# Token halves at four norms, context first at a fifth, shorter GpSimd sums behind two blocks

## The chip, the cores and the metric

The kernel runs on one core of one Trainium2 chip. The metric is the device time of one execution in microseconds (us), the median of three runs. The engines are named as in the profile: PE (TensorE), DVE (VectorE), ACT (ScalarE), POOL (GpSimd), SP (the queue that issues most transfers).

## What is computed

Two network blocks on 256 latent tokens of width 1024; the second also carries 256 context tokens. Cut to what matters here:

```python
h = rms_norm(x, norm_g) * (1 + scale) + shift      # before every projection
x = x + gate * y                                   # after every mixer: the residual
lat = lat + 0.5 * mod[:, 0, 2] * _swiglu(_modulate(lat, ...), w13, w2)   # FFN of 2816 hidden
cx  = cx  + 0.5 * modc[0, 2]   * _swiglu(_modulate(cx,  ...), w13, w2)   # the same weights
```

All of it is float32. `scale`, `shift` and `gate` of each layer come from matrix-vector products of the condition vector with `ada_w` and `mod_w`. The norm's mean runs over the 1024 features of one token, so a norm can't start until every feature of that token has its residual, and tokens do not depend on each other there.

## The kernel before

**Layout.** Activations are held transposed: XT has 8 chunks of 128 features (k = 0 to 7) by 512 tokens, the latent tokens in columns 0 to 255, the context tokens in 256 to 511. Each float32 product is made of three matmuls on rounded halves: weights split into Wh and Wl, activations into Hh and Hl (`three`, L1320: Wh·Hh, Wh·Hl, Wl·Hh).

**Stages.** 17 linear stages run one after the other: even_in, even_out, odd_in, odd_out, ffn0_up, ffn0_down, conv_in, conv_out, ffn1_up, ffn1_down, ffn2_up, ffn2_down, gqa_kv, gqa_q, gqa_out, ffn3_up, ffn3_down (table STAGES, L44). The stages from ffn0_up to gqa_kv work on 512 tokens, the others on 256. A stage is a row of weight tiles. A tile of 2048 columns holds two output blocks by 8 input chunks: 48 matmuls. A tile of an FFN down stage holds half of the hidden chunks of one output block: 33 matmuls, and two tiles make one output chunk. One number per stage in the table, `gemv`, says how many rows of the modulation products DVE takes beside each tile (`modulation_of`, L870): each is two dot products of 1024 elements (`dot`, L855, lines L864 and L867, or one at L861 for the first block).

**The path of a tile.** SP loads it into raw (two slots), ACT copies it, rounded, into Wh (`split`, L527), DVE subtracts to get Wl (L832), PE multiplies. There are two Wh/Wl slots; the next tile is split while PE works on this one, and ACT's split of tile n waits until PE is through with tile n-2.

**A norm.** `splits` (ACT, L561) squares each chunk of XT once its residual is written; POOL adds the squares of the first chunks into tmp[2] (L460, count in SUMMED, L257); PE multiplies that sum and the squares of the remaining chunks with a column of ones into psN (`sum_of`, L1378); DVE makes the means (L897), POOL takes them to the power -1/2 (L452), PE spreads the result over 128 rows (`spread`, L1376), then for each chunk DVE scales (`scaled`, L903), ACT adds the shift and rounds (L586), DVE makes the low part (L919), all helpers' DVE operations under L819. PE's first tile of the next stage takes chunk by chunk. The norm ffn0_up also folds the first block's final norm in (L890 to L894, L467, and at the end 8 rescalings of XT, L921). The residuals are made on DVE in `residual` (L925) and `ffn_down` (L960).

**Order.** Each engine runs one hand-written list, at the end of its block; semaphores connect them. On DVE, the step of a tile is: split of the next tile, modulation products, residual of this tile.

## Time and profile before

| | |
|---|---|
| median of 3 runs | 2079.53 us (2076.51 to 2079.58) |
| the profiled execution, its own time | 2075.76 us |
| its span | 2073.9 us |
| PE busy | 1906.5 us, 92% |
| DVE busy | 1397.0 us, 67% |
| ACT busy | 689.9 us, 33% |
| POOL busy | 128.0 us, 6% |
| granted TensorE clock, mean | 0.965 |
| bytes moved | 315.79 MB, mean 152 GB/s |

Busy shares are means over stages with different limits. A matmul's duration in the trace overlaps with the next one's, so the time per matmul is read from start to start, or as a piece of the chain divided by its instructions.

### The profile page before, as it was taken

To read this page: it belongs to the slowest core of one execution; us is meant where nothing else is said; L and a number is where in the kernel's file an instruction comes from. 1 tells how busy PE (TensorE), PEld (TensorE's weight loads), DVE (VectorE), ACT (ScalarE), POOL (GpSimd) and SP (SyncE) were. 2 spreads that over 40 slices of the span, in tenths; PEclk is the share of its full clock that TensorE was granted. 3 is DMA by queue.
4 is the path that set the end of the run, shared out by engine and by line. 5 is a ranking of instruction groups with operands and counts; after the bars stand their busy time and mean duration, and the time that the engine had idled before them with its cause. 6 is when DMAs were issued, how large, how long until landed. Compare 5 with 4: busy or idle time off the path is not lost.

```text
span 2073.9 us, 26722 instructions
## 1 busy us (share of the span) xinstructions
PE 1906.5 (92%) x10092; PEld 1621.9 (78%) x10092; DVE 1397.0 (67%) x2081; ACT 689.9 (33%) x926; POOL 128.0 (6%) x78
## 2 busy tenths in 40 slices
PE   2986799799999998998999999999999998879998
PEld 2955788688888877876888888778888887669998
DVE  7878899876666666668666666676665226755554
ACT  2454355422222223332222222232222213444432
POOL 2001200200000110003000001100000010010000
PEclk9987899799999999998999999999999999999999
DMA  9843854423443452334333444433343233223444
GB/s 378 319 169 78 227 199 176 174 105 138 152 152 133 157 187 112 136 138 171 118 131 146 152 144 155 178 114 132 148 152 108 96 110 113 83 82 142 168 160 158
DMA packets 75738, 315.79 MB, mean 152 GB/s; under 512 B 19060, under 2 KB 22904, under 8 KB 56344
## 3 DMA queue, kind: packets, MB, share of 16 engines
q1 hardware_dynamic: 75136, 314.15, 42.7%
q8 instruction: 37, 0.61, 0.1%
q10 hardware_dynamic: 536, 0.79, 0.1%
q14 instruction: 29, 0.24, 0.0%
HBM read 313.86 MB, written 1.06 MB: 152 GB/s over the span
## 4 chain that ended last, share of the span: by engine, by line
PE 74%; DVE 18%; ACT 3%; issue 2%; DMA 1%; POOL 1%; SPq 0%; DVEq 0%; ACTq 0%
PE acc L1318 72%; DVE Wl L832 4%; ACT Wh L527 2%; DVE tmp L819 2%; PE psN L1318 1%; DVE psGT L861 1%; DVE psGT L867 1%; DVE psGT L864 1%; DVE najunk L867 1%; DVE najunk L864 1%; DVE small L989 1%; DVE XT L819 1%; DMA afirst<-in_ada_w 1%; PE psN L1380 1%; DVE tmp L1007 1%
## 5 line engine op out<-in xcount | busy, mean ns | idle before, releaser
L1318 PE MATMUL acc<-Hh,Wh 128*128 128x512 f32 (+1 forms) x2320 | 808.4, 348 | 48.7 <-DVE Hl L819 23.3
L1318 PE MATMUL acc<-Hl,Wh 128*128 128x512 f32 (+1 forms) x2320 | 799.5, 345 | 0.0
L1318 PE MATMUL acc<-Hh,Wl 128*128 128x512 f32 (+1 forms) x2320 | 798.9, 344 | 0.0
L832 DVE TENSOR_TENSOR Wl<-raw,Wh 128x2048 fp32r<-128x2048 f32 (+1 forms) x214 | 449.6, 2101 | 270.3 <-ACT Wh L527 270.2
L1318 PEld LDWEIGHTS acc<-Hh,Wh 128*128 128x128 f32 x2320 | 447.9, 193 | 112.9 <-issue 46.7
L527 ACT ACTIVATE Wh<-raw 128x2048 fp32r<-128x2048 f32 (+1 forms) x214 | 374.3, 1749 | 343.0 <-PE acc L1318 329.6
L1318 PEld LDWEIGHTS acc<-Hl,Wh 128*128 128x128 f32 x2320 | 448.5, 193 | 50.4 <-issue 0.7
L1318 PEld LDWEIGHTS acc<-Hh,Wl 128*128 128x128 f32 x2320 | 447.4, 193 | 50.5
L1318 PE MATMUL acc<-hidh,Wh 128*128 128x512 f32 (+1 forms) x704 | 258.6, 367 | 0.9 <-DVE Wl L832 0.9
L1318 PE MATMUL acc<-hidl,Wh 128*128 128x512 f32 (+1 forms) x704 | 258.3, 367 | 0.0
L1318 PE MATMUL acc<-hidh,Wl 128*128 128x512 f32 (+1 forms) x704 | 258.2, 367 | 0.0
L594 ACT ACTIVATE tmp<-acc 128x512 f32<-128x512 f32 (+1 forms) x88 | 47.9, 544 | 454.6 <-PE acc L1318 454.6
L819 DVE SCALAR_TENSOR_TENSOR tmp<-tmp,acc 128x512 f32<-128x512 f32 (+1 forms) x176 | 109.3, 621 | 131.1 <-ACT tmp L594 120.9
L460 POOL TENSOR_TENSOR tmp<-tmp 128x512 f32<-128x512 f32 (+1 forms) x44 | 93.2, 2118 | 1308.4 <-ACT tmp L558 1151.5
L864 DVE SCALAR_TENSOR_TENSOR psGT<-graw,cb 128x1024 f32<-128x1024 f32 x122 | 167.7, 1375 | 0.4
L867 DVE SCALAR_TENSOR_TENSOR psGT<-graw,cb 128x1024 f32<-128x1024 f32 x122 | 154.9, 1270 | 4.2
L1318 PEld LDWEIGHTS acc<-hidh,Wh 128*128 128x128 f32 x704 | 132.4, 188 | 24.8 <-DVE Wl L832 1.1
L1318 PEld LDWEIGHTS acc<-hidh,Wl 128*128 128x128 f32 x704 | 132.4, 188 | 24.0
L1318 PEld LDWEIGHTS acc<-hidl,Wh 128*128 128x128 f32 x704 | 132.4, 188 | 23.9
L956 DVE TENSOR_TENSOR hidl<-tmp,hidh 128x512 f32 (+3 forms) x88 | 55.1, 626 | 71.4 <-ACT hidh L597 71.4
L819 DVE SCALAR_TENSOR_TENSOR XT<-acc,mod,XT 128x256 f32 (+3 forms) x88 | 36.0, 455 | 88.5 <-PE acc L1318 88.5
L597 ACT ACTIVATE hidh<-tmp 128x512 f32 (+3 forms) x88 | 50.9, 578 | 133.5 <-DVE tmp L819 133.5
(222 smaller groups left out, 1187.7 us busy)
## 6 DMA issues: line engine op xcount, KB each, us to landing
raw<-in_ffn_up SPq DMA_DIRECT2D x88, 1024.0 KB, 4.8
graw<-in_mod_w SPq DMA_DIRECT2D x144, 512.0 KB, 5.5
raw<-in_ffn_down SPq DMA_DIRECT2D x64, 704.0 KB, 4.1
graw<-in_ada_w SPq DMA_DIRECT2D x32, 512.0 KB, 5.7
raw<-in_odd_in SPq DMA_DIRECT2D x16, 1024.0 KB, 4.9
raw<-in_even_in SPq DMA_DIRECT2D x12, 1024.0 KB, 7.0
raw<-in_conv_in SPq DMA_DIRECT2D x12, 1024.0 KB, 4.8
afirst<-in_ada_w SPq DMA_DIRECT2D x8, 1024.0 KB, 13.0
```

The lines of the kernel that those rows point to most:

```text
L460: nc.gpsimd.tensor_tensor(tmp[:, 2, 0:n], tmp[:, 0 if k == 1 else 2, 0:n], tmp[:, k % 2, 0:n], ALU.add).then_inc(n_sum, 1)
L527: nc.scalar.activation(Wh[:, half, 0:f], raw[:, slot, 0:f], ACT.Copy).then_inc(hi_ready, 1)
L594: nc.scalar.activation(tmp[:, b, 0:s.tokens], acc[b][0][:, 0:s.tokens], ACT.Tanh, scale=0.5)\
L597: nc.scalar.activation(at3(hidh, t, s.tokens), tmp[:, 3, 0:s.tokens], ACT.Copy).then_inc(ffn_hi, 1)
L819: return nc.vector.scalar_tensor_tensor(out=out, in0=a, scalar=s, in1=b, op0=op0, op1=op1)
L832: nc.vector.tensor_tensor(Wl[:, half, 0:f], raw[:, slot, 0:f], Wh[:, half, 0:f].bitcast(f32), ALU.subtract)\
L861: nc.vector.scalar_tensor_tensor(out=psGT[:, :], in0=graw[:, slot, :], scalar=0.5, in1=cfirst[:, :], op0=ALU.mult, op1=ALU.mult, accum_out ...
L864: nc.vector.scalar_tensor_tensor(out=junk[:, :], in0=graw[:, slot, :], scalar=0.5, in1=cb[:, 0, :], op0=ALU.mult, op1=ALU.mult, accum_out= ...
L867: nc.vector.scalar_tensor_tensor(out=junk[:, :], in0=graw[:, slot, :], scalar=0.5, in1=cb[:, 1, :], op0=ALU.mult, op1=ALU.mult, accum_out= ...
L956: nc.vector.tensor_tensor(at3(hidl, t, c), tmp[:, 3, c], at3(hidh, t, c).bitcast(f32), ALU.subtract)\
L989: link(nc.vector.tensor_reduce(out=out, in_=L[:, u % 2, :, :], op=ALU.max, axis=AX.X))
L1318: return nc.tensor.matmul(out, lhsT, rhs, start=start, stop=stop)
```

## The change

It has five parts.

1. **Halved tokens** at the norms conv_in, ffn1_up, ffn2_up and gqa_kv (`HALVED`). The last output tile of the stage before is computed for the latent tokens first (semaphore lat_done), then for the context tokens. The latent half's residual, last squares, sums, power and spread run while PE is in the context half. The next stage's first two tiles are then taken as: latent tokens of tile 0, of tile 1, context tokens of tile 0, of tile 1, and DVE and ACT do the latent chunks first, then the context chunks. The matmuls concerned have 256 columns in place of 512. The splits of the next stage's first tiles are cut into halves of 1024 columns and put between the chunks.
2. **Context first** at the norm ffn0_up. The context rows' norm is known since the norm odd_in, so the context halves of the first two tiles are normed and multiplied first, and the sums and power of the latent tokens run beside. The 8 rescalings of XT stand after the stage ffn0_up.
3. **Sums** behind even_out and odd_out (`MID`): POOL adds four chunks' squares (3 additions for 5), and PE takes chunks 4 and 5 itself, inside the last tile, after its sixth input chunk.
4. **Products**: conv_out takes 1 modulation row per tile for 2, gqa_out 1 for 0.
5. **Splits** of tile 2 of ffn0_up, ffn1_up and ffn2_up are put behind the tanh of tile 0 on ACT, and before the low part of tile 0 on DVE.

```diff
-    ("conv_out", 4, 16, 0, TOK, 2, "dve"),
+    ("conv_out", 4, 16, 0, TOK, 1, "dve"),
...
-    ("gqa_out", 4, 16, 0, LAT, 0, "dve"),
+    ("gqa_out", 4, 16, 0, LAT, 1, "dve"),
...
-        SUMMED = {"even_in": 6, "odd_in": 5, "ffn0_up": 5, "conv_in": 6, "ffn1_up": 5, "ffn2_up": 6, "gqa_kv": 6, "ffn3_up": 5}
+        SUMMED = {"even_in": 6, "odd_in": 3, "ffn0_up": 3, "conv_in": 6, "ffn1_up": 5, "ffn2_up": 6, "gqa_kv": 6, "ffn3_up": 5}
...
+        HALVED = {n: i for i, n in enumerate(["conv_in", "ffn1_up", "ffn2_up", "gqa_kv"])}
+        LAST = {n: (KC - 2, KC - 1) if n == "ffn1_up" else (KC - 1,) for n in HALVED}
+        CL, CC = slice(0, LAT), slice(LAT, TOK)
```

DVE at a halved norm:

```diff
+                dve.wait_ge(lat_done, l + 1)
+                residual_half(0, CL).then_inc(lat_res, 1)
+                meanwhile()
+                mean(0, psN, lat_ss, l + 1).then_inc(lat_mean, 1)
+                if not ffn:
+                    split(S[name].n0)
+                dve.wait_ge(lat_spread, l + 1)
+                scaled(0, 0, CL, psN).then_inc(lat_t, 1)
+                for k in range(KC):
+                    if k + 1 < KC:
+                        if k > 0:
+                            dve.wait_ge(lat_ready, KC * l + k)
+                        scaled(k + 1, 0, CL, psN).then_inc(lat_t, 1)
+                    if ffn and k < 2:
+                        split_half(S[name].n0, k)
+                    dve.wait_ge(lat_hi, KC * l + k + 1)
+                    low(k, 0, CL).then_inc(lat_ready, 1)
+                    if k in (5, 7):
+                        split_half(S[name].n0 + 1, k // 2 - 2)
+                    if k == 2:
+                        dve.wait_ge(tile_done, s.n0 + s.tiles)
+                        residual_half(1, CC).then_inc(drained["dve"], 1)
+                    if k == 5:
+                        mean(1, psT[1], n_ss, i + 1).then_inc(n_mean, 1)
```

PE at a halved norm, the last tiles of an FFN down stage and the first two of the next stage:

```diff
+                    part(0, 0, CL)
+                    sum_of_sums(name)
+                    part(0, 1, CL).then_inc(lat_done, 1)
+                    part(1, 0, CC, lat_sums).then_inc(tile_done, 1)
+                    lat_spreads(name)
+                    part(1, 1, CC).then_inc(tile_done, 1)
...
+                pe.wait_ge(lo_ready, s.n0 + 1)
+                part(0, CL, lat_ready, KC * l, {3: ctx_sums, 7: ctx_spread})
+                pe.wait_ge(lo_ready, s.n0 + 2)
+                pe.wait_ge(drained["dve"], prev.drained1)
+                part(1, CL, lat_ready, KC * l, {})
+                part(0, CC, h_ready, H0[name], {}).then_inc(tile_done, 1)
+                part(1, CC, h_ready, H0[name], {}).then_inc(tile_done, 1)
```

PE behind even_out and odd_out, and at the norm ffn0_up:

```diff
+                        if k == 5 and X_TO.get(s.name) in MID and t == s.tiles - 1:
+                            sums_between(X_TO[s.name])
...
+            part(0, CC, ctx_ready, 0, range(4))
+            for k in range(KC - 2, KC):
+                pe.wait_ge(n_sq, KC * i + k + 1)
+                ins = sum_of("ffn0_up", tmp[:, k % 2, :], False, k == KC - 1)
+            ins.then_inc(n_ss, 1)
+            part(0, CC, ctx_ready, 0, range(4, KC))
+            pe.wait_ge(lo_ready, s.n0 + 2)
+            pe.wait_ge(drained["dve"], S["odd_out"].drained1)
+            part(1, CC, ctx_ready, 0, range(4))
+            pe.wait_ge(n_rstd, i + 1)
...
+            part(1, CC, ctx_ready, 0, range(4, KC))
+            part(0, CL, h_ready, H0["ffn0_up"], range(KC)).then_inc(tile_done, 1)
+            part(1, CL, h_ready, H0["ffn0_up"], range(KC)).then_inc(tile_done, 1)
```

**The order of the work, place 1: PE between ffn0_down and conv_in.** Before, the last tile runs to its end, then come the squares' sums, the spread, and the first matmul of conv_in:

```order
L1318 MATMUL acc<-hidh,Wl 128x512
L1380 MATMUL psN<-ones,tmp 128x1 [waits n_sq]
L1380 MATMUL psN<-ones,tmp 128x1 x3
L1376 MATMUL psN<-ident,rstd 128x128 [waits n_rstd]
L1376 MATMUL psN<-ident,rstd 128x128 x3
```

Now sums and spread of the latent tokens (psN) stand inside the context half of the last output chunk (hidh, hidl are the FFN's hidden values):

```order
L1523 MATMUL acc<-hidh,Wl 128x256
L1559 MATMUL psN<-ones,tmp 128x1 [waits lat_sq]
L1559 MATMUL psN<-ones,tmp 128x1
L1523 MATMUL acc<-hidh,Wh 128x256
```

```order
L1523 MATMUL acc<-hidh,Wl 128x256
L1675 MATMUL psN<-ident,rstd 128x128 [waits lat_rstd]
L1675 MATMUL psN<-ident,rstd 128x128
L1523 MATMUL acc<-hidh,Wh 128x256 [waits lo_ready]
```

15 matmuls stand between lat_done and the sums, 18 more between the sums and the spread, 33 behind the spread.

**Place 2: DVE at the conv_in norm.** Before, the whole split of tile 1 (2048 columns) stands ahead of the first scaled chunk, and both halves of a chunk follow each other:

```order
L819 SCALAR_TENSOR_TENSOR XT<-acc,mod,XT 128x256 [waits tile_done]
L819 SCALAR_TENSOR_TENSOR XT<-acc,mod,XT 128x256
L897 TENSOR_SCALAR means<-psN 128x4 [waits n_ss]
L819 SCALAR_TENSOR_TENSOR mod<-mod,vec 128x16 [waits g_taken]
L832 TENSOR_TENSOR Wl<-raw,Wh 128x2048 [waits hi_ready,dve_chain]
L819 SCALAR_TENSOR_TENSOR tmp<-XT,mod,psN 128x256 [waits n_spread]
L819 SCALAR_TENSOR_TENSOR tmp<-XT,mod,psN 128x256 x3
L819 SCALAR_TENSOR_TENSOR Hl<-tmp,mod,Hh 128x256 [waits n_hi]
```

Now the latent chunks are alone, with the half splits (128x1024) of tiles 0 and 1 and the context residual between them:

```order
L909 SCALAR_TENSOR_TENSOR XT<-acc,mod,XT 128x256 [waits lat_done]
L909 SCALAR_TENSOR_TENSOR mod<-mod,vec 128x16 [waits g_taken]
L998 TENSOR_SCALAR means<-psN 128x2 [waits lat_ss,dve_chain]
L909 SCALAR_TENSOR_TENSOR tmp<-XT,mod,psN 128x256 [waits lat_spread]
L909 SCALAR_TENSOR_TENSOR tmp<-XT,mod,psN 128x256
L982 TENSOR_TENSOR Wl<-raw,Wh 128x1024 [waits hi_half]
L909 SCALAR_TENSOR_TENSOR Hl<-tmp,mod,Hh 128x256 [waits lat_hi]
L909 SCALAR_TENSOR_TENSOR tmp<-XT,mod,psN 128x256 [waits lat_ready]
L982 TENSOR_TENSOR Wl<-raw,Wh 128x1024 [waits hi_ready]
L909 SCALAR_TENSOR_TENSOR Hl<-tmp,mod,Hh 128x256 [waits lat_hi]
```

Two more half splits follow behind chunks 5 and 7, and the eight context chunks behind those.

**Place 3: DVE in gqa_out.** Before, a tile is a split and its residuals:

```order
L832 TENSOR_TENSOR Wl<-raw,Wh 128x2048 [waits hi_ready]
L819 SCALAR_TENSOR_TENSOR XT<-acc,mod,XT 128x256 [waits tile_done]
L819 SCALAR_TENSOR_TENSOR XT<-acc,mod,XT 128x256
L832 TENSOR_TENSOR Wl<-raw,Wh 128x2048 [waits hi_ready]
L819 SCALAR_TENSOR_TENSOR XT<-acc,mod,XT 128x256 [waits tile_done]
```

Now two dot products and their taking over (graw is the modulation row) stand ahead of every residual:

```order
L922 TENSOR_TENSOR Wl<-raw,Wh 128x2048 [waits hi_ready]
L954 SCALAR_TENSOR_TENSOR psGT,small<-graw,cb 128x1024 [waits g_done,g_loaded1,g_taken]
L957 SCALAR_TENSOR_TENSOR psGT,small<-graw,cb 128x1024 [waits g_half]
L943 TENSOR_TENSOR mod<-small,vec 128x2 [waits g_done]
L909 SCALAR_TENSOR_TENSOR XT<-acc,mod,XT 128x256 [waits tile_done]
```

In conv_out's tiles, which had two such pairs of dot products ahead of the residuals, one pair is left.

## Rows read from the trace of the kernel before

**Rows 1.** Page, part 4: share of the chain that ended last, by engine.

```profile
PE 74%; DVE 18%; ACT 3%; issue 2%; DMA 1%; POOL 1%; SPq 0%; DVEq 0%; ACTq 0%
```

**Rows 2.** Chain in order of time: start us, us, what, instructions.

```profile
409.82 357.83 PE acc L1318 x1551
...
794.90 122.71 PE acc L1318 x540
...
1836.50 23.03 PE acc L1318 x192
```

**Rows 3.** Waits of PE: total us, times, longest us.

```profile
PE psN L1380 <- POOL tmp L460: 35.1, 4, 24.2
PE psN L1376 <- POOL rstd L452: 25.0, 7, 14.9
```

**Rows 4.** Timeline at the conv_in norm: start us, us, engine, instruction, idle before.

```profile
776.27 0.88 DVE L819 SCALAR_TENSOR_TENSOR XT<-acc,mod,XT 128x256 f32<-128x256 f32 x2 [1.56 <-PE acc L1318]
...
777.87 1.05 PE L1380 MATMUL psN<-ones,tmp 128*128 128x1 f32 x8 [1.63 <-ACT tmp L558]
...
780.27 0.65 PE L1376 MATMUL psN<-ident,rstd 128*128 128x128 f32 x4 [1.35 <-POOL rstd L452]
...
784.79 0.77 PE L1318 MATMUL acc<-Hh,Wh 128*128 128x512 f32 x1 [3.88 <-DVE Hl L819]
...
808.84 1.09 ACT L543 ACTIVATE cv_proj<-acc 128x512 f32<-128x512 f32 x2 [7.99 <-PE acc L1318]
```

**Rows 5.** Timeline of DVE in the odd_in norm, 256-column chunks.

```profile
231.56 0.48 DVE L819 SCALAR_TENSOR_TENSOR tmp<-XT,ada,psN 128x256 f32<-128x256 f32 x1
...
232.47 0.48 DVE L819 SCALAR_TENSOR_TENSOR tmp<-XT,ada,psN 128x256 f32<-128x256 f32 x1
```

**Rows 6.** Groups by form: count, busy us, mean ns, idle before.

```profile
L832 DVE TENSOR_TENSOR Wl<-raw,Wh 128x2048 fp32r<-128x2048 f32 x150 | 345.5, 2304 | 169.6 <-ACT Wh L527 169.5
...
L864 DVE SCALAR_TENSOR_TENSOR psGT<-graw,cb 128x1024 f32<-128x1024 f32 x122 | 167.7, 1375 | 0.4
```

**Rows 7.** Timeline at the end of even_out.

```profile
218.20 2.03 DVE L861 SCALAR_TENSOR_TENSOR psGT<-graw,cfirst 128x1024 f32<-128x1024 f32 x1
...
221.99 3.57 PE L1380 MATMUL psN<-ones,tmp 128*128 128x1 f32 x16 [0.93 <-ACT tmp L558]
```

**Rows 8.** Timeline around the ffn0_up norm: last residual, second tile drained.

```profile
396.51 0.87 DVE L819 SCALAR_TENSOR_TENSOR XT<-acc,ada,XT 128x256 f32<-128x256 f32 x2
...
434.59 0.60 ACT L594 ACTIVATE tmp<-acc 128x512 f32<-128x512 f32 x1 [3.99 <-PE acc L1318]
```

**Rows 9.** Timeline around the ffn1_up norm: sums, last residual, second tile drained.

```profile
965.24 1.05 PE L1380 MATMUL psN<-ones,tmp 128*128 128x1 f32 x8 [0.88 <-POOL tmp L460]
...
967.77 1.65 DVE L819 SCALAR_TENSOR_TENSOR XT<-acc,mod,XT 128x256 f32<-128x256 f32 x4
...
1003.18 0.60 ACT L594 ACTIVATE tmp<-acc 128x512 f32<-128x512 f32 x1 [6.37 <-PE acc L1318]
```

**Rows 10.** Timeline in gqa_out: a split, the last residual, POOL.

```profile
1844.29 2.29 DVE L832 TENSOR_TENSOR Wl<-raw,Wh 128x2048 fp32r<-128x2048 f32 x1 [1.13 <-ACT Wh L527]
...
1859.56 0.88 DVE L819 SCALAR_TENSOR_TENSOR XT<-acc,mod,XT 128x256 f32<-128x256 f32 x2 [1.46 <-PE acc L1318]
...
1850.40 3.42 POOL L460 TENSOR_TENSOR tmp<-tmp 128x256 f32<-128x256 f32 x2 [3.22 <-ACT tmp L558]
```

**Rows 11.** Windows: length, PE, PEld, DVE, ACT, POOL busy (instructions), granted clock, DMA share, GB/s.

```profile
785.00:788.00 3.00, 3.00 (x8) 2.38 (x9) 2.96 (x8) 1.62 (x4) 0.00 (x0) 0.56 0.82 336
788.00:796.00 8.00, 7.96 (x34) 5.91 (x33) 7.67 (x20) 3.84 (x9) 0.00 (x0) 1.00 0.00 0
371.00:397.00 26.00, 19.49 (x152) 19.09 (x152) 25.72 (x32) 9.95 (x15) 10.66 (x5) 0.96 0.65 235
```

**Rows 12.** Timeline of PE, 256 columns just after a long idle.

```profile
232.02 0.42 PE L1318 MATMUL acc<-Hl,Wh 128*128 128x256 f32 x1
232.23 0.41 PE L1318 MATMUL acc<-Hh,Wl 128*128 128x256 f32 x1
```

More of the change, by code:

```diff
@@ L747, in _ @@
             splits(S["odd_out"])
-            norm("ffn0_up")
+            context_first()
             ffn_up(S["ffn0_up"])
@@ L962, in step @@
                 def step(t, u, i):
+                    if halved(s) and isinstance(t, int) and t == s.tiles - 1:
+                        modulation_of(s, t, u, i)
+                        return
                     next_split(s, t, u, i)
@@ L1546, in _, with part @@
             last.then_inc(tile_done, 1)
+            pe.wait_ge(n_pow, 1)
+            for b in range(QB):
+                ins = spread(psT[1][:, LAT + b * P:LAT + (b + 1) * P], rctx, b)
+            ins.then_inc(ctx_spread0, 1)
             linear(S["odd_out"], begin=1)
-            norm("ffn0_up")
-            linear(S["ffn0_up"])
+            s, i = S["ffn0_up"], NORMS["ffn0_up"]
+            def part(t, c, ready, base, chunks):
+                for k in chunks:
+                    pe.wait_ge(ready, base + k + 1)
+                    for j in range(2):
+                        last = three(acc[t][j][:, c], (s.n0 + t) % SPLIT, j * KC + k, Hh[:, k, c], Hl[:, k, c], k == 0, k == KC - 1)
+                return last
```

318 lines of the change are left out of this document (278 added, 40 removed).

## The prediction

> **What bounds the kernel now.** I read the chain of waits first: matmuls of L1318 and the other PE work hold 74% of it, DVE 18% [rows 1]. So time comes off only where PE stands still, or where it gets fewer or cheaper matmuls. Its pieces in order of time [rows 2] show two cadences: 122.71 us for 540 matmuls of 512 columns, 0.227 us each (0.231 over the longer piece before it, 357.83 us for 1551), and 23.03 us for 192 matmuls of 256 columns, 0.120 us each. In the list of PE's waits [rows 3] the norms stand on top: 35.1 us for POOL's sums, 25.0 us for POOL's powers. Of these 24.2 and 14.9 are single waits early in the program that the change does not touch. Then I read each norm on the timeline. At conv_in [rows 4] the last matmul ends where the residual starts, 776.27; PE then does 1.05 us of sums and 0.65 us of spread, and starts conv_in at 784.79, 8.5 us later; the second tile is drained at 808.84. The first tile runs at DVE's pace, four operations a chunk. This shape stands at ffn2_up and gqa_kv too; at ffn1_up and ffn0_up the gap is longer.
>
> **The unit of the walk.** For each norm I walk the new order from the last old point that is not changed to the drain of the next stage's second tile. A 256-column chunk costs DVE 0.91 us (231.56 to 232.47) [rows 5]. A split of 2048 columns has a mean of 2.30 us [rows 6]; a half split is at least half of that, 1.15, and I take 1.2. A dot product alone takes 1.23 us; the mean is 1.375 [rows 6], and beside POOL's additions it is 2.03 [rows 7].
>
> **Conv_in (halved).** PE's last two FFN tiles are 66 matmuls of 0.231 us and 0.95 of sums, so they began at 776.25 - 16.2 = 760.05. New: the latent half is 33 x 0.120 = 4.0, the summed squares 0.95 and up to 0.3 of waiting for POOL's last addition, 4.0 again: lat_done at 769.3. The context half is 7.9, with 0.5 of sums and 0.35 of spread in it: PE is free at 778.0, 1.7 us later than before. The latent chain (residual, square, sums, mean, power, spread) ends with the spread at 774.0, bounded by where PE's list has the spread, so it is hidden. From there DVE has 8 latent chunks, 7.3; the residual of the context half and a mean, 0.6; four half splits, 4.8; and about 1.5 in which it waits for ACT, which does its own four half splits and two squares between the same chunks. That is 14.2 us: tile 1 is split at 788.2. PE starts its first chunk about 778.4 (it needs both halves of tile 0's split) and is through with the latent tokens of tile 0 just before 788.2. Then nothing holds it: 144 matmuls x 0.120 = 17.3, the second tile is done at 805.5. The context chunks need DVE until 796.2, and PE wants the first at 794.0 and the last at 799.1: covered. Drained before at 808.84, done 0.1 earlier. **Gain 3.2.** The price of the halving itself is inside: 162 pairs of 256 in place of 512 columns, 0.0127 each, 2.1 us.
>
> TensorE's back-to-back cost is where a page can be weighed. The rows say that 2 x 0.120 against 0.227 is 12.7 ns per pair [rows 2]. The Trainium skill, page "TensorE: Matmul & The Clock Gate", section "Back-to-back issue gap", gives 262 cycles for 256 columns and 518 for 512, so 6 cycles or 2.5 ns per pair. By the page each halved norm would gain 1.6 us more and the whole sum some 6 us; the row is of this kernel's own stream, weight loads included, and I take it.
>
> **Ffn2_up** is the same walk. **Gain 3.2.** The split of tile 2 now waits for tile 0's tanh: 0.6 + ACT 1.9 + DVE 2.2, and the low part 0.7, some 5.5 us behind tile 0, while PE has 5.8 us of tile 1's context half. Cost nothing; without that cover up to 1 us.
>
> **Gqa_kv** is the same walk, but its second tile (the values) has 256 columns already, so 48 pairs less pay 12.7 ns, 0.6. PE's sums over the keys move from the second to the third token block and ACT has 2.0 us of copies for 2.9 us of matmuls there: hidden. The values' mean and power come later against PE's list, by my walk within 0.2 us of where PE asks for them. **Gain 3.8.**
>
> **Ffn1_up (halved, behind conv_out).** PE's last conv_out tile ended at 965.24 - 0.88 = 964.4, and DVE, with two modulation rows a tile, came to its residual only at 967.77 [rows 9]. With one row DVE is no longer late. New: last tile from 964.4 - 48 x 0.233 = 953.2; latent half 5.8; here the summed squares wait for POOL until about 960.5 and take 1.0; context half 5.8 and 1.0 of sums in it; spread 0.35: 969. DVE has 8 chunks 7.3, two half splits 2.4, two residuals and a mean 1.1, first chunk's latency 0.9, waits for ACT 0.8: tile 1 can go at about 982. Plus 17.3 is 999.2; before 1003.18 [rows 9]. **Gain 3.9.**
>
> **Even_out.** POOL's last two additions lay on DVE's two dot products of the last tile, 2.29 and 2.03 us for 1.23 [rows 7]: 1.8 back. The last tile ends 3.9 us later on PE (12 sum products, of which 8 came behind the tile before, and a wait for ACT's squares), at 217.8 before DVE asks at 218.5: hidden. PE's 16 rows of sums took 3.57 us at the low clock after a long idle [rows 7]; with little idle they take 2.1, as 8 take 1.05 at conv_in [rows 4]: 1.5 more. **Gain 3.3**, handed through odd_in, which DVE bounds.
>
> **Ffn0_up (context first).** The last residual comes at 395.5 in place of 396.51 [rows 8]: 2.0 less for the dot products, 0.4 more for two small operations that now stand ahead of odd_out, 0.5 for the first context chunk. ACT's four squares end at 398.0, the first context chunk is ready at 399.0. DVE then has 7 chunks 6.4, ACT's split of tile 1 in between about 1.0, DVE's split 2.2, four means 0.8: 409.5. PE: 0.7, half of tile 1's context 2.9, spreads 1.1 (all 414.2), the rest 2.9 (417.1), latent halves 5.8 and 5.8: 428.7, and 0.4 until tile 2 is split. Before 434.5 [rows 8]: 5.4. The 8 rescalings of XT, 3.2 us of DVE, now stand ahead of the second tile's split of ffn0_down, where PE's first tile takes 33 x 0.231 = 7.6 and DVE needs of it about 3.5 for the last hidden chunk and 1.6 for the split: 2.5 free, minus 0.6. **Gain 4.8.**
>
> **Gqa_out** pays. DVE's period of a tile there is 5.76, PE's own: a split begins at 1844.29, the last residual at 1859.56 [rows 10]. New: split 2.2, two dot products and taking over 2.9, residual 0.8 is 5.9, so the last residual would be at 1844.29 + 3 x 5.9 - 0.8 = 1861.2 with no POOL. POOL's five additions (3.42 us for two [rows 10]) fall on these products and make each about 0.9 longer: 1865.7. **Loss 6.1.** The ends: 1.6 if no addition lands on a product, 7 if each costs what it did at even_out.
>
> **Sum**: 3.3 + 4.8 + 3.2 + 3.9 + 3.2 + 3.8 - 6.1 = 16.1 us, against the profiled execution's own 2075.76: 2059.7. The median of the runs is 3.8 above that execution, so 2079.53 - 16.1 = **2063.4**. A measurement of this kernel can tell about 0.2%, 4 us, from no change.
>
> **Rivals.**
> (a) *DVE and ACT bound the halved tiles more than I walked.* All halves of a norm hang on a ping-pong of DVE and ACT with half splits between; half a microsecond per half split and a late latent chain cost 2 us per halved norm, and 1.5 at ffn0_up. For it: DVE is busy 7.7 of 8 us while it norms [rows 11]. Against it: the operations are all ones that the trace shows. Gain 6.5: 2073.
> (b) *Gqa_out hides the products*, POOL's additions falling elsewhere. Then 4.5 more: 2058.9.
> (c) *The moves are given back*: the odd_in and gqa_q stages have fixed partners, or the halves' order just moves the wait from the spread to lo_ready. Within 4 us of no change: 2078.
> (d) *The slow side: TensorE's clock.* Between 785 and 788 the granted clock was 0.56 after idle stretches, and 1.00 from 788 on [rows 11]; at the low level (1.2 GHz) 256 columns start 0.213 us apart [rows 12], not 0.120. In the new latent part of tile 0 PE is busy only two thirds of 10 us. If the clock falls there and stays low, each of the dense 256-column matmuls behind costs 0.093 more. From 43 such matmuls per norm (4.0 us of the 16.1) the gain is gone; over 96 of them, up to the end of tile 0, at four norms it is 36 us: 2099. Against it: from 371 to 397 PE was busy 19.49 of 26 us, with pauses, at 0.96 [rows 11]. The Trainium skill, "TensorE: Matmul & The Clock Gate", section "HAM oscillation", warns of just this, gaps in PE's work that bring the low clock again and again; the long gaps that did so in the rows are the ones the change removes.
>
> **How the numbers follow.** Forecast 0.57 (own range 2060 to 2068), (a) 0.20, (b) 0.10, (c) 0.07, (d) 0.06. The predicted time is the forecast's. The range leaves out (c), (d) and the tails of (a) and (b): 2057 to 2073.5. Faster by over 0.2% (below 2075.4): all of the forecast and (b), nearly all of (a), a little of (c): 0.88. Same: 0.06. Slower: 0.06.
>
> **What would show it.** Right: PE starts conv_in, ffn2_up and gqa_kv within 1 us of its last FFN matmul, and its idle time before POOL's powers shrinks by about 7 us; tile 1 of conv_in drained some 29.3 us behind what is now 776.27, less the shift so far, in place of 32.5; conv_out's DVE no longer behind PE; the last residual of gqa_out about 6 us later against that stage's start, with dot products of 2 us beside POOL's additions; 256-column matmuls 0.120 us apart. Wrong: a granted clock near half in the first tiles of a halved norm (d), first tiles that take over 12 us for the latent half (a), or gqa_out's tiles still 5.8 us apart (b).

## The result, and the profile of the changed kernel

| | before | after |
|---|---|---|
| median of 4 runs each, taken beside each other | 2078.02 us | 2058.38 us (2057.45 to 2062.44) |
| the profiled execution, its own time | 2075.76 us | 2057.45 us |
| its span | 2073.9 us | 2055.7 us |
| PE busy | 1906.5 us | 1912.6 us |
| granted TensorE clock, mean | 0.965 | 0.974 |

The ratio is 0.991, 95% interval 0.9892 to 0.9927: faster by 0.9%. The medians are 19.6 us apart, the profiled executions 18.3; the prediction had 16.1 and 2063.4, its range went from 2057 to 2073.5. So the measured median lies 1.4 us inside the range's lower edge, and below the 2060 at which the forecast's own range began.

The chain that ended last, by engine (page, part 4): PE's share is up, DVE's down from 18% [rows 1], and DMA and SP now have some.

```profile
PE 75%; DVE 14%; ACT 4%; issue 3%; DMA 2%; POOL 1%; SPq 1%; ACTq 0%; DVEq 0%; POOLq 0%
```

The waits of PE (total us, times, longest), five lines of the list. Beside the two long waits early in the program, 24.5 and 14.9 us, which are as before, POOL's sums have 4.1 us left (L1695 holds the halved norms') of the 10.9 in [rows 3], and its powers 2.9 of 10.1. DVE's chunks stand on top at the norms.

```profile
PE psN L1679 <- POOL tmp L479: 26.7, 2, 24.5
PE acc L1523 <- DVE Hl L909: 21.2, 13, 4.1
PE psN L1675 <- POOL rstd L471: 17.8, 4, 14.9
PE acc L1523 <- DVE Wl L922: 17.3, 21, 2.8
...
PE psN L1695 <- POOL tmp L479: 1.9, 4, 0.6
```

Timeline at the conv_in norm, against [rows 4]. PE has the latent sums and the latent spread inside the context half of the last FFN tile, and starts conv_in at 772.14 after 0.40 us of idle time, where it stood 3.88 us for DVE. Two more pauses, of 0.67 and 1.01 us, are all there is in the first tile.

```profile
764.89 0.50 PE L1559 MATMUL psN<-ones,tmp 128*128 128x1 f32 x4
767.46 0.38 PE L1675 MATMUL psN<-ident,rstd 128*128 128x128 f32 x2
772.14 0.39 PE L1523 MATMUL acc<-Hh,Wh 128*128 128x256 f32 x1 [0.40 <-DVE Wl L982]
775.21 0.39 PE L1523 MATMUL acc<-Hh,Wh 128*128 128x256 f32 x1 [0.67 <-DVE Hl L909]
...
793.08 1.09 ACT L568 ACTIVATE cv_proj<-acc 128x512 f32<-128x512 f32 x2 [4.50 <-PE acc L1523]
798.84 1.09 ACT L568 ACTIVATE cv_proj<-acc 128x512 f32<-128x512 f32 x2 [2.87 <-PE acc L1523]
```

From the first to the second tile drained are 5.76 us for 48 matmuls of 256 columns, 0.120 each: the cadence of [rows 2], so a pair still costs 12.7 ns more than one of 512.

**A ledger.** Every weight tile is copied once by ACT (`Wh<-raw`; where it goes in two halves the first counts), so the start of that copy can be compared tile by tile between two traces. Between the norms the difference stays the same to 0.03 us over hundreds of microseconds, but for single copies that start 0.1 to 0.35 early or late and catch up; it moves at the places of the change, and where the clock differs. That gives what each place brought. Gains in us against the kernel before (minus is a loss):

| place (start of the copy that ends it, before) | predicted | measured |
|---|---|---|
| even_out, odd_in (DVE's split at 369.41) | 3.3 | 0.9 |
| ffn0_up's norm (448.08) | 5.4 | 6.7 |
| first tiles of ffn0_down (675.35) | -0.6 | -1.1 |
| conv_in (842.45) | 3.2 | 3.9 |
| ffn1_up (1016.67) | 3.9 | 5.6 |
| ffn2_up (1401.84) | 3.2 | 4.0 |
| gqa_kv (1762.41) | 3.8 | 4.7 |
| gqa's attention, up to gqa_out's second split (1842.34) | 0 | -2.7 |
| gqa_out (1861.10) | -6.1 | -3.4 |
| everything else | 0 | -0.3 |
| sum | 16.1 | 18.3 |

The even_out row is the 0.54 at that split and the 0.3 us by which this execution was already late before the first changed place; that 0.3 is the last row but one, which also holds 0.8 gained at the ffn3_up norm and 0.7 lost again in the last tiles. Two rows hold what the prediction did not have: gqa's attention, whose code is the same, and gqa_out. Windows of the changed kernel (length, busy us of PE, PEld, DVE, ACT, POOL with instructions, granted clock, DMA share, GB/s), at conv_in, at ffn1_up, and at the end of gqa's attention:

```profile
772.00:782.00 10.00, 8.16 (x60) 7.39 (x61) 8.67 (x19) 4.50 (x9) 0.70 (x1) 1.00 0.43 157
959.00:970.00 11.00, 9.11 (x59) 8.48 (x59) 9.13 (x19) 5.38 (x11) 0.69 (x1) 0.84 0.29 121
1811.00:1816.00 5.00, 4.71 (x19) 4.14 (x20) 1.52 (x3) 2.03 (x2) 0.00 (x0) 0.66 0.02 3
```

The clock is full (2.4 GHz) through conv_in's first tile, where it was 0.56 for 3 us before [rows 11]; 0.50 is the other level, 1.2 GHz. The kernel before also had a mean of 0.52 at ffn2_up (1347 to 1357) and of 0.50 at gqa_kv (1723 to 1733), and the change has the full clock there too. In the kernel before, the low stretch at ffn2_up was the longer (10 us; at conv_in 7 us, 781 to 788, mean 0.52), yet both places gained the same to 0.1. So the clock's share in the gain is likely small; no run separates it. In the change the clock drops at ffn1_up, and in the attention, where the profile of before had none. There eight matmuls of the last mix take 3.12 us; all the mixes before it take 1.98.

```profile
1806.38 1.99 PE L1523 MATMUL psN<-gP,gtok 128*128 128x256 f32 x8 [0.69 <-ACT gP L716]
...
1811.29 3.12 PE L1523 MATMUL psN<-gP,gtok 128*128 128x256 f32 x8 [0.69 <-ACT gP L716]
```

Gqa_out, against [rows 10]: a split, the two dot products beside POOL, the last residual.

```profile
1831.16 1.77 DVE L954 SCALAR_TENSOR_TENSOR psGT<-graw,cb 128x1024 f32<-128x1024 f32 x1
...
1833.02 1.59 DVE L957 SCALAR_TENSOR_TENSOR psGT<-graw,cb 128x1024 f32<-128x1024 f32 x1
...
1835.57 2.28 DVE L922 TENSOR_TENSOR Wl<-raw,Wh 128x2048 fp32r<-128x2048 f32 x1
...
1841.36 0.87 DVE L909 SCALAR_TENSOR_TENSOR XT<-acc,mod,XT 128x256 f32<-128x256 f32 x2
```

### The profile page after: what moved, and what is told of

Its sections match the earlier page's. It is cut to its first block, busy times and chain, and to the rows that moved or that the text cites. A ratio compares the mean times of both kernels' runs of the same rounds, so it can differ in the third digit from the quotient of the medians.

```text
span 2055.7 us, 28138 instructions
## 1 busy us (share of the span) xinstructions
PE 1912.6 (93%) x10802; PEld 1655.6 (81%) x10802; DVE 1399.8 (68%) x2096; ACT 693.5 (34%) x938; POOL 116.1 (6%) x78
## 3 DMA queue, kind: packets, MB, share of 16 engines
HBM read 313.86 MB, written 1.06 MB: 153 GB/s over the span
## 4 chain that ended last, share of the span: by engine, by line
PE 75%; DVE 14%; ACT 4%; issue 3%; DMA 2%; POOL 1%; SPq 1%; ACTq 0%; DVEq 0%; POOLq 0%
PE acc L1523 72%; DVE Wl L922 3%; ACT Wh L552 2%; DVE tmp L909 2%; PE psN L1523 1%; DMA afirst<-in_ada_w 1%; DVE Hl L909 1%; DVE XT L909 1%; DVE psGT L951 1%; DVE psGT L954 1%; DVE Wl L982 1%; SPq L431 1%; DMA raw<-in_ffn_down 1%; POOL tmp L479 0%; PE psGT L1523 0%
## 5 line engine op out<-in xcount | busy, mean ns | idle before, releaser
L1523 PE MATMUL acc<-Hh,Wh 128*128 128x256 f32 (+1 forms) x2464 | 834.5, 339 | 47.5 <-DVE Hl L909 21.2
L1523 PE MATMUL acc<-Hl,Wh 128*128 128x256 f32 (+1 forms) x2464 | 823.9, 334 | 0.0
L1523 PE MATMUL acc<-Hh,Wl 128*128 128x256 f32 (+1 forms) x2464 | 823.4, 334 | 0.0
L922 DVE TENSOR_TENSOR Wl<-raw,Wh 128x2048 fp32r<-128x2048 f32 (+1 forms) x207 | 433.5, 2094 | 245.1 <-ACT Wh L552 244.8
L1523 PEld LDWEIGHTS acc<-Hh,Wh 128*128 128x128 f32 x2464 | 476.1, 193 | 107.0 <-issue 36.7
L1523 PEld LDWEIGHTS acc<-Hl,Wh 128*128 128x128 f32 x2464 | 476.5, 193 | 44.4 <-issue 0.7
L1523 PEld LDWEIGHTS acc<-Hh,Wl 128*128 128x128 f32 x2464 | 476.0, 193 | 43.8
L552 ACT ACTIVATE Wh<-raw 128x2048 fp32r<-128x2048 f32 (+1 forms) x207 | 360.9, 1744 | 338.0 <-PE acc L1523 308.4
L1523 PEld LDWEIGHTS acc<-hidh,Wh 128*128 128x128 f32 x770 | 144.8, 188 | 24.3 <-DVE Wl L922 3.1
L1523 PEld LDWEIGHTS acc<-hidl,Wh 128*128 128x128 f32 x770 | 144.9, 188 | 21.1
```

What stands on the lines that cost most here:

```text
L552: nc.scalar.activation(Wh[:, half, 0:f], raw[:, slot, 0:f], ACT.Copy).then_inc(hi_ready, 1)
L922: nc.vector.tensor_tensor(Wl[:, half, 0:f], raw[:, slot, 0:f], Wh[:, half, 0:f].bitcast(f32), ALU.subtract)\
L1523: return nc.tensor.matmul(out, lhsT, rhs, start=start, stop=stop)
```

## The experiments

What each kernel gained against the kernel before at the places that differ between them, by the same ledger, from one profiled execution each (us; "first part" is all up to 448.08):

| kernel | first part | ffn0_down | conv_in | ffn1_up | ffn2_up | gqa_kv | attention | gqa_out |
|---|---|---|---|---|---|---|---|---|
| the change | 7.2 | -1.1 | 3.9 | 5.6 | 4.0 | 4.7 | -2.7 | -3.4 |
| rows_back | 7.7 | -1.1 | 3.9 | -3.1 | 4.0 | 4.7 | -2.8 | 0.0 |
| before_rows | -0.6 | 0.0 | 0.0 | 4.7 | -0.6 | 0.6 | -1.2 | -3.4 |
| conv_whole | 8.0 | -1.1 | 0.0 | 5.7 | 4.0 | 4.7 | -2.6 | -3.4 |
| sums_five | 2.5 | -1.1 | 3.9 | 5.8 | 3.9 | 4.7 | 0.0 | -3.4 |
| rows_ffn2 | 7.8 | -1.1 | 3.9 | 6.0 | 4.0 | 4.7 | -4.4 | 0.0 |
| rows_ffn2_all | 6.7 | -1.1 | 3.9 | 4.8 | 3.9 | 4.7 | -2.9 | 0.0 |
| rescale_beside | 7.3 | 0.0 | 3.9 | 3.8 | 3.9 | 4.7 | -1.3 | -3.4 |
| warm_ffn3 | 7.9 | -1.1 | 3.9 | 6.0 | 3.9 | 4.7 | -4.3 | -3.4 |
| bias_later | 6.4 | -1.1 | 3.9 | 6.0 | 4.0 | 4.7 | -4.6 | -3.4 |
| combined | 7.2 | 0.0 | 3.9 | 6.0 | 4.0 | 4.7 | -2.6 | 0.0 |
| mixes_warm | 7.9 | 0.0 | 3.9 | 6.0 | 4.0 | 4.7 | -5.4 | 0.0 |
| mixes_warm_one | 6.7 | 0.0 | 3.9 | 5.9 | 3.9 | 4.7 | 0.0 | 0.0 |

A column that reads the same in ten kernels is a term known to 0.1 us. Three columns scatter: ffn1_up, the attention, and the first part, which is the same code in the change and in nine of the kernels below (all but before_rows, sums_five and bias_later) and reads 6.7 to 8.0 there. In all three the clock is at work; in the first part a late load is too. That is also why the medians below carry 2 to 3 us of their own: the profiled executions, and the places in them, say more. By the medians' intervals alone only before_rows, combined and mixes_warm_one can be told from the change.

**rows_back.** The change with its modulation rows put back.

```diff
-    ("conv_out", 4, 16, 0, TOK, 1, "dve"),
+    ("conv_out", 4, 16, 0, TOK, 2, "dve"),
-    ("gqa_out", 4, 16, 0, LAT, 1, "dve"),
+    ("gqa_out", 4, 16, 0, LAT, 0, "dve"),
```

> The changed kernel with its modulation rows where they were before: conv_out 2 a tile, gqa_out 0. Theory (the rows pay at gqa_out and are needed at ffn1_up): gqa_out's tiles are 5.8 us apart again and its last residual stands 3.9 us earlier against the stage's start; but four dot products now stand ahead of the latent residual of conv_out's last tile, which PE finishes 5.8 us sooner than a whole tile, so the latent residual comes about 6 us later than in the changed kernel and ffn1_up's second tile is drained 5 to 6 us later: 2058.4 - 3.9 + 5.5 = 2060. Rival (halving alone makes ffn1_up's gain, the context half covers the late dot products): ffn1_up loses at most 1 us and the kernel is at 2055.5.

Measured: median 2061.0 (ratio 0.9919, 0.9906 to 0.9933), span 2061.2 for 2055.7. Gqa_out gets 3.4 back; ffn1_up loses 8.7 where 5 to 6 was expected, so the theory held and its rival fell. PE's waits in this kernel's last conv_out tile and the first of ffn1_up:

```profile
952.99 0.61 PE L1695 MATMUL psN<-ones,tmp 128*128 128x1 f32 x4 [4.66 <-POOL tmp L479]
966.11 0.36 PE L1523 MATMUL acc<-Hh,Wh 128*128 128x256 f32 x1 [1.73 <-DVE Hl L909]
970.30 0.58 PE L1523 MATMUL acc<-Hh,Wh 128*128 128x256 f32 x1 [0.65 <-DVE Hl L909]
```

The late residuals delay POOL's sums by 4 us as well, the first chunk comes at 966.11 for 959.41, and PE then runs most of the tile at the low clock. With two rows a tile the halves at ffn1_up are worse than the whole norm (-3.1 against 0).

**before_rows.** The same two lines changed in the kernel before.

> The kernel before with only the modulation rows moved: conv_out 1 a tile for 2, gqa_out 1 for 0. Theory: conv_out's last residual is no longer late against PE, ffn1_up gains 2.5 us; gqa_out's tiles go from 5.76 to 6.6 us apart and its last residual comes 3.9 us later, as in the changed kernel: 2078.0 - 2.5 + 3.9 = 2079.4. Rival (the size in the prediction, 6.1 at gqa_out): 2081.6. Second rival (without halves the late residual at conv_out costs nothing, since POOL's sums hold PE there): no gain at ffn1_up, 2081.9.

Measured: median 2075.13 beside 2077.71 (0.9989, 0.998 to 0.9998). Ffn1_up gains 4.7, gqa_out loses 3.4. So the rows alone give 4.7 of the 5.6 us at ffn1_up; the halves give 1 us on top of them, and only with them. The expected 2.5 was short by two causes. The last residual comes 3.4 us earlier (965.05, less 0.65 of shift, for 967.77), and the squares' sums behind it, which start sooner after PE's last matmul, run at the higher clock: 1.95 us for the 3.57 that such 16 rows took there in the kernel before.

```profile
967.42 1.95 PE L1380 MATMUL psN<-ones,tmp 128*128 128x1 f32 x16 [1.63 <-ACT tmp L558]
```

**conv_whole.** The change, conv_in's norm whole.

```diff
-        HALVED = {... ["conv_in", "ffn1_up", "ffn2_up", "gqa_kv"])}
+        HALVED = {... ["ffn1_up", "ffn2_up", "gqa_kv"])}
```

> The changed kernel with the norm conv_in taken whole as before, the other three halved. Theory (each halved norm gains on its own): conv_in's second tile is drained 3.9 us later and everything behind it moves by as much, 2058.4 + 3.9 = 2062.3; the granted clock falls to about 0.56 for some us at the start of conv_in, where the changed kernel has 1.00. Rival (what one norm gives is picked up or given back by a later fixed partner): less than 2 us at the end.

Measured: conv_in gains 0.0 for 3.9, the other changed places keep theirs to 0.1, as the theory had it; median 2060.29 (0.9914, 0.99 to 0.9928), span 2058.6, 2.9 above the change's, whose first part was 0.8 us slower. The clock dips again where conv_in begins:

```profile
778.00:782.00 4.00, 4.00 (x12) 3.20 (x13) 3.93 (x10) 1.82 (x4) 0.00 (x0) 0.65 0.65 270
```

**sums_five.** The change with five additions on POOL behind even_out and odd_out, and PE's sums only at the norm.

```diff
-        SUMMED = {"even_in": 6, "odd_in": 3, "ffn0_up": 3, ...
+        SUMMED = {"even_in": 6, "odd_in": 5, "ffn0_up": 5, ...
-        MID = ("odd_in", "ffn0_up")
+        MID = ()
```

> The changed kernel with POOL adding six chunks' squares (5 additions) behind even_out and odd_out as before, and no sums on PE inside the last tile. Theory (POOL's additions lengthen the dot products of the last tile by 0.9 us each, and nothing else): the last residual of even_out and of odd_out comes 1.5 to 2 us later; at odd_in the load of the second weight tile, not the norm, sets the time, so only 0 to 1 us is lost there; at ffn0_up 1.8 us: 2058.4 + 2.3 = 2060.7. Rival (as the prediction had it, both norms are paid in full): 3.3 + 2.0, 2063.7. Second rival (context chunks cover the latent residual at ffn0_up): under 1 us in all.

Measured: 4.7 us less up to 448.08: 1.5 of it by odd_out's start, 3.1 at the norm ffn0_up, 0.1 ahead of both. The theory (2.3) was short by half; the rival (5.3) is nearer, and that the median came out at the theory's 2060.7 is luck. So of the change's 6.7 us at that norm 3.1 belong to the sums and 3.6 to taking the context first. The 3.1 are the last residual 1.6 us later, the means 1.9, and then a first stretch of tiles at the low clock:

```profile
408.00:415.00 7.00, 7.00 (x48) 7.00 (x48) 3.00 (x8) 0.51 (x1) 1.34 (x2) 0.76 0.62 225
```

The change has 0.95 from 401 to 415. The span is 2056.1 all the same and the median 2060.84 (0.9925, 0.9911 to 0.9938): this execution lost nothing in gqa's attention, where the change lost 2.7. The attention's code is the same in both; what differs, as far as the traces show, is the time at which it begins.

**rows_ffn2.** Gqa_out's four rows beside the last four tiles of ffn2_down.

```diff
-    ("ffn2_down", 2 * KC, W2H, 0, TOK, 0, "dve"),
+    ("ffn2_down", 2 * KC, W2H, 0, TOK, 1, "dve"),
...
-    ("gqa_out", 4, 16, 0, LAT, 1, "dve"),
+    ("gqa_out", 4, 16, 0, LAT, 0, "dve"),
...
-                if s.gemv:
+                if s.gemv and (not s.from_t or isinstance(t, int) and t >= s.from_t):
```

> The changed kernel with gqa_out's four modulation rows taken beside the last four tiles of ffn2_down (which has none), gqa_out 0. Theory (the rows cost 3.4 us at gqa_out, where a tile gives DVE 5.8 us, and nothing where a tile gives 7.7): nothing moves up to the end of ffn2_down and at gqa_kv, gqa_out's tiles are 5.8 us apart, everything behind it is 3.4 us earlier: 2058.4 - 3.4 = 2055.0. Rival (the products ahead of ffn2_down's latent residual make it late, as four of them did at conv_out): gqa_kv loses 2 us or more, 2057.

Measured: median 2054.66 (0.9893, 0.9877 to 0.9908), span 2053.3. Gqa_out costs 0.0 for 3.4, gqa_kv keeps 4.7: a tile of ffn2_down hides the rows wholly.

**rows_ffn2_all.** Conv_out without rows too, ffn2_down with eight.

> As rows_ffn2, and conv_out without rows, ffn2_down with eight (tiles 8 to 15, written out). Theory (conv_out's latent residual still stands behind a tile's products): ffn1_up gains another 1.0 us, since POOL's additions, no longer beside products, end sooner too: 2054. Rival (POOL's sums alone set the norm there): nothing more than rows_ffn2, 2055.0.

Measured: median 2055.39 (0.9895, 0.988 to 0.991), ffn1_up gains 4.8 for rows_ffn2's 6.0. The first chunk does come earlier: the first matmul of ffn1_up stands 0.8 us sooner against the shift so far (959.05 + 9.48 for 958.82 + 10.55). Then PE is at the low clock from 960 to 971 and loses 2 us. The theory was right on the rows (0.8 of the 1.0) and still gave no gain.

**rescale_beside.** The eight rescalings of XT moved into ffn0_up's last two tiles.

```diff
                     modulation_of(s, t, u, i)
+                    if s.name == "ffn0_up" and isinstance(t, int) and t >= FC - 2:
+                        for k in range((t - FC + 2) * 4, (t - FC + 2) * 4 + 4):
+                            stt(XT[:, k, CL], XT[:, k, CL], V("final_g", k), psT[1][:, CL], ALU.mult, ALU.mult)
```

> The changed kernel with the eight rescalings of XT in the last two tiles of ffn0_up, four in each, where DVE waits for the tanh, in place of behind the stage. Theory (they hold the split of ffn0_down's second tile, 1.14 us): the first tiles of ffn0_down keep ffn0_up's offset and all behind is 1.1 us earlier: 2057.3. Rival (they now delay the splits of ffn0_up's last tiles or the last hidden chunk by as much): no change, 2058.4.

Measured: ffn0_down costs 0.0 for 1.1, as expected; median 2056.03 (0.9894, 0.9878 to 0.9909). The profiled span is still 2055.7, since ffn1_up gave 3.8 where rows_ffn2 had 6.0. The windows of the two kernels there, this one first:

```profile
959.00:970.00 11.00, 10.19 (x49) 9.75 (x48) 7.96 (x16) 4.81 (x10) 0.69 (x1) 0.54 0.24 84
```

```profile
958.00:969.00 11.00, 8.79 (x58) 8.23 (x58) 9.34 (x19) 5.78 (x12) 0.69 (x1) 0.84 0.33 133
```

At a mean clock of 0.54 PE gets 49 matmuls done in 11 us, at 0.84 it does 58 and still has pauses. The code of this norm is the same in both.

**warm_ffn3.** 24 throwaway matmuls on PE at the norm ffn3_up.

```diff
+                        for _ in range(count):
+                            nc.tensor.matmul(psT[1][:, 0:LAT], Wh[:, v, 0:P], Wh[:, v, P:P + LAT], start=True, stop=True, ...)
```

> The changed kernel with 24 throwaway matmuls of 256 columns on PE (8 ahead of the last squares' sums, 6 ahead of the power, 10 behind the spread) at the norm ffn3_up, results unused. Theory (the low granted clock after the idle stretch costs the first tile of ffn3_up about 1 us, DVE's chunks bound the rest): the granted clock in the first tile is near 1.00 in place of 0.75 and the stage's first tanh comes 1 us earlier against the last residual: 2057.4. Rival (the throwaway matmuls run at the low clock themselves and stand in the way of sums and spread): 0 to 1.5 us slower. Second rival (the clock costs all of its 2 us there, the first tile hangs on PE): 2056.4.

Measured: median 2056.46 (0.9901, 0.9886 to 0.9917); nothing can be said for it. The first 8 still run at the full clock, the others at the low one, and the granted clock stays low until 1850, where the theory had near 1.00:

```profile
1842.00:1850.00 8.00, 6.91 (x33) 6.44 (x32) 5.35 (x11) 3.55 (x6) 0.71 (x1) 0.59 0.20 57
```

Between gqa_out's end and ffn3_up's third tile this execution gained 1.6 us on the kernel before, but sums_five gained 1.3 there and before_rows 1.4 without any such matmul. The same 24 matmuls are in combined and the two kernels behind it, where gqa_out has no rows and PE's gap is shorter. There the mean clock of the same window is 0.79, 0.79 and, in mixes_warm_one, full:

```profile
1842.00:1850.00 8.00, 8.00 (x59) 7.20 (x59) 6.07 (x15) 3.44 (x7) 0.00 (x0) 1.00 0.27 115
```

Rows_ffn2, with the shorter gap and without the matmuls, has 0.59. The three gain 1.1, 1.2 and 1.6 at this norm, the kernels without the matmuls between 0 and 1.4, so a gain in time is not shown there either.

**bias_later.** The neighbour bias loaded 4, 2, 6 a tile for 4, 4, 4.

> The changed kernel with the loads of the neighbour bias (twelve, on SP's queue ahead of odd_in's weight tiles) split 4, 2, 6 over even_out's last three tiles in place of 4, 4, 4. Theory (SP is 3 us late with the load of odd_in's second tile, and ACT's split and DVE's wait for it eat most of what the shorter sums give at even_out): ACT's split of that tile no longer waits for its load, DVE's 2.45 us of waiting for it before the odd_in norm goes, odd_in's first matmul is 1 to 2 us earlier. Rival (the bias itself then comes too late for the work beside the norm): DVE waits there for as long, and odd_in ends no earlier. At the end of the program at most 1 us either way.

Measured: median 2058.1 (0.9903, 0.9886 to 0.9919), no gain. ACT no longer waits for the second tile, but DVE's 2.45 us for the split have only turned into 2.02 us for the spread. From the means to the first chunk DVE needs 4.38 us; in the change 4.82. So in that execution the late load cost 0.4 us, not 2. It can cost more: in the nine other kernels with the change's code up to here the same stretch took 4.0 to 6.5 us, the longest in mixes_warm_one, where the means came early (222.83) and DVE then waited for ACT's split until 227.15.

```profile
225.29 0.16 DVE L1047 TENSOR_SCALAR means<-psN 128x4 f32<-128x4 f32 x1 [4.33 <-PE psN L1679]
229.67 0.87 DVE L909 SCALAR_TENSOR_TENSOR tmp<-XT,ada,psN 128x256 f32<-128x256 f32 x2 [2.02 <-PE psN L1675]
```

**combined.** rows_ffn2, rescale_beside, warm_ffn3, and throwaway matmuls at ffn1_up.

```diff
+                    for k in (0, 1, 4, 5, 6):
+                        beside[k] = lambda name: warm_up(s, 1)
+                    beside[2] = lambda name: warm_up(s, 9)
...
                         lat_spreads(X_TO[s.name])
+                        warm_up(S[X_TO[s.name]], 12)
```

> rows_ffn2, rescale_beside and warm_ffn3 in one, and throwaway matmuls at the ffn1_up norm too (12 of 256 columns behind the latent spread, 9 behind chunk 2, one behind each of chunks 0, 1, 4, 5, 6 of the first tile's latent half). Theory (the stretch of low granted clock that starts between 958 and 965 in every run and lasts 3 to 10 us is made by PE's pauses there, and costs ffn1_up 0.8 to 3 us): no granted clock under 0.9 between 955 and 975, ffn1_up gains at least 6 us against the kernel before where the runs so far have 3.9 to 6.0; with 3.4 from gqa_out's rows, 1.1 from the rescalings and 0.7 from ffn3_up: 2052.5. Rival (the throwaway matmuls only take the place of the pauses, DVE's chunks set the first tile whatever the clock): ffn1_up as in the changed kernel, 2053.2. Second rival (they stand ahead of chunks that are ready and push them back): ffn1_up gains under 5 us, 2054 or more.

Measured: median 2050.98 beside 2077.66 (0.9864, 0.9847 to 0.988), span 2049.7. The clock at ffn1_up is full:

```profile
955.00:970.00 15.00, 13.43 (x107) 12.60 (x106) 11.74 (x25) 6.81 (x14) 1.78 (x2) 1.00 0.34 112
```

It is so in all three kernels with these matmuls, while the change and its eight variants without them all have a stretch at the low level between 953 and 981. The gain there is 6.0, no more than rows_ffn2 had with a dip of 3 us. So a short dip costs little, 0 to 0.3 (5.6 to 6.0 in the six kernels with one): that DVE's chunks set the pace of that tile is the likely reason, not shown by a run of its own. The long ones, as in rescale_beside, cost 2. The matmuls hold the clock, and are an insurance more than a gain: the expected 6 at ffn1_up came, but not from the clock as the theory had it.

**mixes_warm** and **mixes_warm_one.** Combined, with throwaway matmuls in the attention's pauses: four (three at the last mixes), then one.

```diff
             def turn(a, u):
+                if a is gqa and u > 2 and (u % 2 == 1 or u >= 14):
+                    keep_warm(psT[u % 2], u - 1, 4)
                 pe.wait_ge(a.normed, u + 1)
```

> The kernel combined, with throwaway matmuls of 256 columns in PE's pauses of gqa's attention too: four ahead of every second unit's transposes (of every one from unit 14 on), three ahead of the last two mixes, written into the bank that the transposes use next. Theory (the stretches of low granted clock inside the attention, which are there in most runs behind the change and cost 0 to 4.5 us between the values and gqa_out's second tile, come from PE's pauses of 1.1 us per unit): no granted clock under 0.9 between 1785 and 1815, and the stretch from gqa_q's first tile to gqa_out's second costs at most 1.3 us in place of 2.6: 2051.0 - 1.5 = 2049.5. Rival (half a microsecond of matmuls a pause is too little): the low stretches stay, 2051. Second rival (the throwaway matmuls delay the transposes): a unit takes longer than 2.85 us, 2053 or more.

> As mixes_warm, with one throwaway matmul in each place in place of four or three. In mixes_warm the four took 1.9 us (they are float32, two instructions each, 0.24 us apart), so two units took 6.14 us for 5.70. Theory: one takes 0.47 us of a pause of 1.06, two units take 5.70 us again, and the clock stays up as it did in mixes_warm: from gqa_q's first tile to gqa_out's second 0 to 1.3 us are lost, 2049.5. Rival (one is too little to hold the clock): low stretches between 1785 and 1815 again, 2051 as combined.

Measured: mixes_warm 2054.52 (0.9887, 0.9871 to 0.9904), as its second rival had it. The clock holds, but four float32 matmuls take 1.9 us of a pause of 1.06 and the attention loses 5.4. mixes_warm_one: median 2048.87 beside 2077.61 (0.9868, 0.9852 to 0.9885), span 2047.0, the attention loses 0.0. The windows over the attention, of mixes_warm_one first, then of rescale_beside:

```profile
1785.00:1815.00 30.00, 26.68 (x136) 19.25 (x135) 17.08 (x45) 13.70 (x26) 0.00 (x0) 1.00 0.00 1
```

```profile
1785.00:1815.00 30.00, 23.23 (x110) 15.81 (x109) 16.15 (x47) 14.40 (x29) 0.00 (x0) 1.00 0.01 1
```

The second shows that a dip is not certain: without the added matmuls this execution had its only one at 1770, and the kernel before none at all. Of the ten traces of the change and its variants without them, one lost nothing in the attention; neither of the two kernels with them had a dip there. That they keep the clock up is shown for the profiled executions, no more; one of mixes_warm_one's four runs took 2053.2 at a mean clock of 0.976, where the other three have 0.979 or 0.980. Whether the last version beats combined can't be told, their intervals overlap. Both beat the two kernels of this study: they end at 0.988 and 0.9885, and the change's begins at 0.9892.

## Why the prediction was right, and where it was not

**The number.** The median came 5.0 us below the 2063.4. The sum was 2.2 of it. The other 2.8 was the step from the profiled execution to the median: 3.8 in the kernel before's first three runs, 0.9 in the change's four. The forecast's mechanism held; its closeness in the sum owes something to terms that offset (below), and the measured 2058.4 being near rival (b)'s 2058.9 is chance, since no product was hidden.

**The mechanism held.** PE starts the three norms behind an FFN within 1 us, its waits for POOL's powers shrank by 7.2 us (25.0 to 17.8), the second tile of conv_in is drained 28.6 us behind the old residual's place (776.27 less the shift of 6.06, to 798.84), where 29.3 was foretold, and conv_whole takes exactly this norm's gain away again.

**The three FFN norms** (3.2, 3.2, 3.8) were each 0.7 to 0.9 short. The walk had tile 1's latent start at 788.2; its last half split ended at 781.21, or 787.27 on the old clock. From the first latent chunk (767.88) to there are 13.3 us for the walk's 14.2. "About 1.5 in which it waits for ACT" was too large: the waits add up to 1.0. The other 0.4 is DVE's own operations, 12.3 for 12.7. The 17.3 us for the 144 matmuls behind it was right.

**Ffn1_up** (3.9, measured 5.6): the sum was short and its reason incomplete. "With one row DVE is no longer late" was a clause in the walk; before_rows shows it to be 4.7 of the 5.6, and rows_back shows that without it the halves lose 3.1. The two edits can't be priced apart: four dot products ahead of the latent residual use up the 5.8 us of context half that is to hide the chain.

**Ffn0_up** (5.4, measured 6.7; 5.7 to 7.0 in the nine other kernels with this code): the context-first order was priced about right. Of the shorter sums, "2.0 less for the dot products" was 1.6 in the residual; sums_five has 3.1 in all, the rest in the means and the clock. The context-first order has no run of its own: its 3.6 is what the sums leave. Nor has part 5, the moved splits.

**Ffn0_down** (-0.6, measured -1.1): the rescalings were costed with 2.5 us of slack, of which the loss leaves 2.1.

**Even_out** (3.3, measured 0.9): the term was too large, and by how much differs from execution to execution. The last residual came 1.8 us earlier, as said. "At the low clock after a long idle; with little idle they take 2.1" did not come in the change: the 16 rows of sums still took 3.58 us, at a clock of 0.50.

```profile
220.49 3.58 PE L1679 MATMUL psN<-ones,tmp 128*128 128x1 f32 x16 [2.23 <-ACT tmp L585]
```

In the nine other kernels with the same code up to here these rows took 3.57 us twice and 1.95 to 2.56 seven times; in combined

```profile
221.03 1.95 PE L1693 MATMUL psN<-ones,tmp 128*128 128x1 f32 x16 [1.63 <-ACT tmp L586]
```

and this place, counted as in the ledger, gained 0.6 to 2.6 us there. So the step can come out as the prediction had it, with the clock; what it left out altogether is the late load of the second weight tile, for which DVE then waits (3.0 us in combined, 4.2 in mixes_warm_one, which had the fast sums and gained 0.6). In none of the ten did the place give 3.3. Sums_five puts the shorter sums at 1.5 here, from one execution of each.

**Gqa_out** (-6.1, measured -3.4): "about 0.9 longer" for a product beside POOL was read at even_out, where POOL's additions have 512 columns. Here they have 256, and the six products of the last three tiles were longer by 0.54, 0, 0.54, 0.36, 0.52 and 0.34, 2.3 in all in place of 4.5. The other 0.5 is DVE's tile without that, 5.7 us for the 5.9 of the walk. The Trainium skill, page "GPSIMD Engine Reference", section "Key points", says that GpSimd shares its SBUF interfaces with VectorE, with contention for DVE instructions that have two SBUF inputs, as a dot product has; the trace agrees (1.77 us beside an addition, 1.23 alone).

**Rival (d), the clock,** was given 0.06 as a catastrophe of 36 us at all four norms. It never came at conv_in, ffn2_up and gqa_kv as halved. It is real at ffn1_up, where PE's first halved tile has more pauses (59 matmuls in 11 us): 0 to 2 us. And it came where the prediction did not look, in the attention, which the change does not touch but whose start it moves: 0 to 4.6 us. That the moved start is the cause is not shown; before_rows, whose start moved by 4 us, lost 1.2 there. The Trainium skill, page "TensorE: Matmul & The Clock Gate", section "A second HAM failure mode: psum-queue depth-cycling", tells of short idles between groups of matmuls that make the clock swing. The traces agree in this: with pauses of 1.07 us per two units the clock fell in the attention in nine of the ten traces of the change and its variants, and in neither of the two with throwaway matmuls in the pauses.

**The other rivals.** (a), DVE and ACT bounding the halved tiles more than walked, fell: the tiles took less than the walk gave them. (b), products hidden at gqa_out, is halfway: no product is hidden, each is lengthened by less. (c), gains given back, is true of single places only: of even_out's, and of the halves at ffn1_up without the moved rows.

**The sum** came out 2.2 us short by terms that offset: the five norms gave 5.4 more than said and gqa_out cost 2.7 less, even_out gave 2.4 less, ffn0_down and the rest took 0.8, and the attention 2.7.
